# Wider weight transfers for pairs 6 to 13 of a one-core mixture-of-experts layer

## What is computed

```
for each expert e (w_up 1024 x 2048, w_down 1024 x 1024, float32):
    hu  = x[frames of e] @ w_up[e] + b_up[e]
    act = min(glu, 7) * sigmoid(1.702 * min(glu, 7)) * (clip(lin, -7, 7) + 1)
    y   = (act @ w_down[e] + b_down[e]) * gate
x = x + sum of y over the experts of each frame
```

## Time and profile before

| | before |
|---|---|
| median of 3 runs | 1032.74 us (1032.35 to 1033.14) |
| profiled execution | 1033.05 us, of which the profile's span is 1030.9 us |
| granted TensorE clock | 0.997 |
| busy: TensorE matmul / weight load | 975.4 us (95%) / 394.8 us (38%) |
| busy: VectorE / ScalarE / GpSimd | 202.9 / 115.5 / 12.8 us |
| transfers | 425.02 MB, 412 GB/s over the span |
| chain that ended last | TensorE 51%, DMA 47% |

### The profile page before, as it was taken

The page is one execution under the profiler, slowest core; times in us unless marked ns, Lnnn a source line. Parts: engine busy times, 40 slices in busy tenths (PEclk is TensorE's granted clock), DMA queues, the critical chain, the costliest instruction groups (busy, mean ns, idle before and its releaser), DMA issues.

```text
span 1030.9 us, 10966 instructions
## 1 busy us (share of the span) xinstructions
PE 975.4 (95%) x4512; PEld 394.8 (38%) x4512; DVE 202.9 (20%) x487; ACT 115.5 (11%) x246; POOL 12.8 (1%) x26
## 2 busy tenths in 40 slices
PE   9999999999999999998998989999999979898997
PEld 5446553434343434342433224342423324232432
DVE  0556132121212121212111211211111211211112
ACT  2427101010101010100000000100001000100000
POOL 0200000000000000000000000000000000000000
PEclk9999999999999999999999999999999999999999
DMA  9955999999999999999999999999999999999996
GB/s 362 417 206 240 407 371 431 428 435 430 423 435 428 434 432 435 428 430 431 440 427 428 433 423 427 430 432 432 435 430 432 430 436 430 428 432 426 428 430 278
DMA packets 25062, 425.02 MB, mean 412 GB/s; under 512 B 3888, under 2 KB 4656, under 8 KB 7888
## 3 DMA queue, kind: packets, MB, share of 16 engines
q1 hardware_dynamic: 24656, 424.18, 97.0%
q10 hardware_dynamic: 384, 0.54, 0.1%
HBM read 423.65 MB, written 1.05 MB: 412 GB/s over the span
## 4 chain that ended last, share of the span: by engine, by line
PE 51%; DMA 47%; another core or an unknown queue 1%; issue 0%; DVE 0%; SPq 0%; ACT 0%; POOLq 0%; POOL 0%; DVEq 0%
DMA everything<-in_w_moe 46%; PE psum L1481 20%; PE psum L1521 12%; PE psum L1141 4%; PE psum L1405 3%; PE psum L1274 3%; PE psum L1103 2%; PE psum L1366 2%; PE psum L1133 1%; PE psum L1116 1%; PE psum L1356 1%; PE psum L1124 1%; DMA everything<-in_w_in 1%; PE psum L1414 0%
## 5 line engine op out<-in xcount | busy, mean ns | idle before, releaser
L1481 PE MATMUL psum<-everything 128*64 128x512 f32 x2048 | 452.2, 598 | 19.4 <-DMA everything<-in_w_moe 19.3
L1481 PEld LDWEIGHTS psum<-everything 128*64 128x64 f32 x2048 | 143.9, 138 | 312.3 <-issue 281.3
L1521 PE MATMUL psum<-everything 128*64 128x512 f32 x1024 | 232.4, 597 | 30.1 <-DMA everything<-in_w_moe 30.1
L1521 PEld LDWEIGHTS psum<-everything 128*64 128x64 f32 x1024 | 74.1, 136 | 174.0 <-issue 170.9
L1068 DVE TENSOR_SCALAR everything<-psum 128x512 f32<-128x512 f32 x32 | 22.2, 692 | 402.5 <-PE psum L1481 402.5
L782 DVE TENSOR_TENSOR everything<-psum,everything 128x512 f32<-128x512 f32 (+1 forms) x38 | 25.0, 663 | 315.0 <-PE psum L1366 297.9
L1405 PE MATMUL psum<-everything 128*128 128x512 f32 x126 | 61.0, 605 | 0.0
L1366 PEld LDWEIGHTS psum<-everything 128*128 128x128 f32 x480 | 54.7, 192 | 12.2 <-issue 12.2
L734 ACT ACTIVATE everything<-everything 128x512 f32<-128x512 f32 x32 | 20.2, 631 | 344.6 <-DVE everything L1068 344.6
L1366 PE MATMUL psum<-everything 128*128 128x128 f32 x480 | 57.6, 278 | 0.0
L755 ACT ACTIVATE everything<-psum 128x256 f32<-128x256 f32 (+1 forms) x48 | 20.1, 454 | 204.4 <-PE psum L1521 204.4
(11 more groups left out here) (165 smaller groups left out, 311.9 us busy)
## 6 DMA issues: line engine op xcount, KB each, us to landing
everything<-in_w_moe SPq DMA_DIRECT2D x71, 4096.0 KB, 47.2
everything<-in_w_moe SPq DMA_DIRECT2D x41, 2048.0 KB, 18.9
everything<-in_w_moe SPq DMA_DIRECT2D x14, 1024.0 KB, 9.4
everything<-in_w_in SPq DMA_DIRECT2D x3, 2048.0 KB, 26.1
everything<-in_w_out SPq DMA_DIRECT2D x2, 2048.0 KB, 11.4
everything<-in_w_moe SPq DMA_DIRECT2D x8, 512.0 KB, 19.9
everything<-in_w_mem_kv SPq DMA_DIRECT2D x1, 2048.0 KB, 16.9
everything<-in_w_in SPq DMA_DIRECT2D x3, 512.0 KB, 7.3
```

The costliest lines, as they stand in the source:

```text
L1481: mm = pe.matmul(psum[r:r + SLOTS, bank], XT[:, k, r:r + SLOTS], weights[i][:, column:column + N], start=first and k == 0 and j >= half, s ...
L1521: mm = pe.matmul(psum[r:r + SLOTS, DOWN_BANKS[n]], actT[:, 2 * i + k, r:r + SLOTS], slot[:, column:column + N], start=i == 0 and k == 0, s ...
```

## The change

For pairs 6 to 13 (the seventh to the fourteenth) SyncE issues three transfers of 8 MB in place of six of 4 MB. A transfer fills four slots. On the side of SBUF these are 64 KB in a row in each partition; in HBM they are two blocks, so each partition gets two rows of 32 KB whose addresses lie 4 MB apart. It is issued once all four slots have been used. Its completion raises `two_in[d]`; `two_in[d + 1]` and the semaphores of `credit` are raised by SyncE at once, which is in order because TensorE waits for `two_in[d]` of the same four chunks first. Bytes, slots, TensorE's program and all other transfers stay.

```
+    WIDE_FROM = 6
...
+        four_slots = [ring[:, s:s + 4, :].rearrange("p (o s) c -> p o (s c)", o=2) for s in range(0, RING, 4)]
...
+            def pair_in_thirds(q, p):
+                for g in range(TWOS // 2):
+                    d = 2 * g
+                    wait_used(q, 2 * d + 3)
+                    sp.dma_start(four_slots[g], w_moe[bass.ds(p * TWOS + d, 2)].rearrange("o r c -> r o c")).then_inc(two_in[d], 16)
+                    sp.sem_inc(two_in[d + 1], 16)
+                    credit(d)
+                    credit(d + 1)
...
-            with sp.Fori(4, PAIRS - 2) as q:
+            with sp.Fori(4, WIDE_FROM) as q:
                 pair(q, q)
+            with sp.Fori(WIDE_FROM, PAIRS - 2) as q:
+                pair_in_thirds(q, q)
             pair_before_last()
```

## The result

| | before | changed |
|---|---|---|
| median of 10 runs each | 1033.09 us | 1034.71 us (1033.92 to 1036.71) |
| ratio | | 1.0019, 95% interval [1.0011, 1.0027] |
| profiled execution / span | 1033.05 / 1030.9 us | 1034.44 / 1032.2 us |
| granted TensorE clock | 0.997 | 0.982 |

The change is slower by 1.6 us. That is 0.1 us outside the range forecast (1031.0 to 1034.6), and the interval excludes both the forecast of no effect and a gain. The forecast of 1032.5 us was counted from 1032.74, the median of three runs; that of ten is 1033.09, so 0.35 of the 2.2 us by which it missed is the base.

What follows compares the result with a forecast made beforehand. The prediction took the saturated DMA queue of weights (431 GB/s in pairs 6 to 13) as the bound, with TensorE waiting for it. All terms were 0 except seams at -0.2 us: 1032.5 us from 1032.74, range 1031.0 to 1034.6.

Steps and rivals of the forecast that it cites:

- the later issue: Pairs 6 to 13: each wide transfer waits for its fourth slot, yet the queue never runs dry: 0 us.
- SyncE's 24 issues: Issues removed, 24 of 48 at 0.333 us each, 8 us of a mostly idle SyncE: gain 0.
- the seams: Between weight transfers: 24 seams fewer give 0 to 1.7 us, taken as 0.2 us gained.
- the jump of 4 MB in HBM: Between a partition's two rows: pace unchanged, 0 us; bounds 2.2 us gained at 433 GB/s, 4.3 us lost at 427.
- The rule of the Trainium skill on rows 4 MiB apart: Within rival 2: such rows copied at 103 GB/s against 207; halved pace in pairs 6 to 13 gives 1499 us, 2%.
- The three waits of pair 6: TensorE waits for wide transfers 3.7, 5.6 and 4.7 us; from pair 7 on two waits, sum 6.6 us per pair: 0.
- TensorE enters the last pair as caught up as before: Pairs 14 and 15, after the wide transfers: 6.6 us of slack in pair 14 absorbs any lateness, 0 us.
- my three signs of being wrong: Pair period other than 58.3 us, DMA share below 0.99, or a weight wait over 2 us in pair 15.
- the term for the clock: After TensorE's waits: low-clock spells, even three a pair, cost 5.0 us, less than the slack of 6.64: 0.
- rival 3: TensorE becomes the bound: spells cost 10.1 us a pair, which takes 61.8 instead of 58.31 us, total 1060; 1%.
- rivals 2 and 3: Rival 2: HBM jump slows pairs 6 to 13 to 427 GB/s, 4.3 us later, 1037.0; 9%. Rival 3: own line.
- The bounds behind the range: Run spread 0.4 us either way, seams 1.7 down, pace 1.9 up: 1030.6 to 1034.8, drawn in to 1031.0 and 1034.6.

Runs made afterwards that it cites:

- e9: Changed kernel with the last third of pair 13 sent as two 4 MB transfers, the other 23 wide ones kept: 1033.45 us, ratio 0.9999 against the kernel before.
- e1: Changed kernel with wide transfers for pairs 6 to 12 only, pair 13 in six doubles again: 1033.35 us, ratio 0.9999 against the kernel before.
- e8: Changed kernel with pair 14 wide too and five overwritten matmuls in the wait ahead of its chunk 8: 1040.31 us, ratio 1.0073 against the kernel before.

## Why the prediction was wrong

*Right:* that the stream is the limit in pairs 6 to 13, 431 GB/s at a share of 1.00, both before and after. *Right:* that the later issue never empties the queue; the landing time was 37.6 us median against some 39 forecast, and the pace held (the last two waits ahead of chunk 8 ended at 846.59 and 904.87, 58.28 us apart). *Right:* that SyncE's 24 issues and the seams are worth nothing that shows, and that the jump of 4 MB in HBM costs nothing: e9 has 23 such transfers and neither loss nor gain to within 0.1%. The rule of the Trainium skill on rows 4 MiB apart (DMA: Bandwidth & Descriptors, Latency and other measured facts) did not bite here, where only the two rows of one partition are that far apart: 431 GB/s in the earlier trace rows and 431 now. The three waits of pair 6, forecast as 3.7, 5.6 and 4.7 us, were 3.62, 3.79 and 4.61; the middle one was shortened by a slow spell in the group before it (15.65 us for chunks 0 to 3, which need 13.8). In later pairs the spell after chunk 8 swallowed most of the waits at chunk 4.

*The step that failed* is "TensorE enters the last pair as caught up as before, because it has 6.6 us of slack in pair 14. 0 us." I compared the slack of a pair with nothing. The lateness to be made up could be had from the text: the last third is worked off from the moment that all its four chunks are there, two chunks and a turn later than before. By the profile of the last wide pair that is 8.6 us with the spell and 7.2 without. Pairs 14 and 15 together hold 7.5 us. So the reserve was spent to within 0.3 us without a spell and overdrawn by 1.1 us with it, and the forecast of "no term for the end" rested on that tie without saying so. None of my three signs of being wrong could see it: the pace held, the share held, and in pair 15 the waits did not grow but went away. The one that did show it was chunk 9 of the last pair, forecast near 1012.3 and no longer held up by the weights. It ran in the group that starts at 1013.74.

*The second failure* is the term for the clock: "Hidden: 0." A spell is hidden as long as a later wait for weights can shrink. After the wait at 904.87 there is none. There the 1.4 to 3.0 us come on top of a lateness that has already used up the slack. My rival 3 had the clock in it, but priced it by the period of a pair, three spells against the slack of a pair, and asked for 2.2 us per wait. The question was what a single spell costs behind the last wait. The mechanism was thus outside all my cases, and slower stood only in rivals 2 and 3, for other reasons. Only the size, 1.6 us, stayed under the bound of 2.1 that I had called no change.

Two slips changed nothing in this. The bounds behind the range were counted from two bases, 1030.6 from 1032.74 and 1034.8 from 1032.5; from the forecast alone the lower one is 1030.4. And the rate of 423 GB/s or more holds from the seventh slice of the earlier trace rows on, as the sixth has 371.

## What to carry to other kernels

A stream that is saturated hides what the consumer does only as long as the consumer still has waits ahead of it. Before enlarging transfers, work out how late the last enlarged one leaves the consumer and set that against the waits that remain up to the end. Coarse transfers belong in the middle of a stream, with fine ones behind the last. Here two pairs of fine ones were too few (1.6 us lost) and three were enough (e1), so leave more than the sum says, for a slow clock. And ask first what there is to gain: with 21 or 23 wide transfers and no loss at the end (e1, e9) the kernel was as fast as before, and no faster.

## What the hardware showed that I had not expected

After a wait for weights of some 4.6 us or more, a stretch at the lower clock level (1.2 instead of 2.4 GHz) followed every time, 37 times in the profiles of the kernels with wide transfers: where a group of 16 records came next, it took between 5.0 and 6.6 us in place of 3.65. After waits of 3.8 us some groups took 3.65 us (611.12 and 788.60 in e8). The same wait of 4.60 us cost 1.36 us in one execution of the changed kernel (5.01) and 2.97 in another (6.62), so its price is not a constant of the program. Filling the wait with matmuls whose result nobody reads kept the group behind it at 3.65 us in three profiles out of three.
